# Sums of a norm taken as one-column matmuls, roots on 128x4 numbers, and their spreading over the partitions by transposes

## The chip, the cores and the metric

The kernel runs on one core of one Trainium2 chip. The metric is the device time of one execution in microseconds (us); the time quoted is the median of three executions. All data are 32-bit floats.

## The reference, cut to what matters

Two layers work on 256 context tokens and 256 latent tokens of width 1024. Each layer has two sub-layers, and each sub-layer ends in the norm of its own output, an addition to the stream, and the norm of the new stream:

```python
def rms_norm(x, g):
    y = x * lax.rsqrt(jnp.mean(jnp.square(x), axis=-1, keepdims=True) + 1e-6)
    return y * g

# end of the mixing sub-layer and start of the FFN sub-layer, for latent and context tokens alike
x = x + mod[2] * rms_norm(y, g_post_mix)
h = rms_norm(x, g_pre_ffn) * (1 + mod[4]) + mod[3]
# end of the FFN sub-layer and start of the next layer
x = x + mod[5] * rms_norm(conv_ffn(h), g_post_ffn)
h = rms_norm(x, g_pre_mix) * (1 + mod[1]) + mod[0]
```

In the second layer only latent tokens are needed after its mixing, so its boundaries work on 256 tokens and not on 512.

## The kernel before, in words

Activations are kept transposed: channels on the 128 partitions, tokens along the free dimension. The stream `x` is 8 tiles of 128 channels x 512 tokens, and so are `h` (as a high part `hh` and a low part `hl`) and the sub-layer's output. A projection goes over units of weights (512 KB each, one DMA of the SP queue into a ring of seven buffers). ACT rounds a unit to `whi` (`hi`, L443), DVE makes the rest `wlo` (`lo`, L842), and PE multiplies `whi` with both parts of the activations and `wlo` with the high part (`part`, L1499; in the first pairs after a boundary, where it follows the tiles of `h` one by one, `tile_part`, L1529). Two output tiles, a pair, stand in two banks of PSUM (banks 0 and 1, or 2 and 3) and are then evacuated.

A boundary is the end of the projection `out` or `down` and the start of the next projection. There are four: `out` and `down` of layer 0 (512 tokens), `out` of layer 1 (256 tokens), and the last, `down` of layer 1 (256 tokens), after which only the stream is stored. At each the kernel needs, for every token, sums over 1024 channels, that is, over partitions and over 8 tiles. With y the branch and s its scaled form, they are the sum of y squared, of s squared, and of x times s. From them it gets the root of the branch (`root1`), and with the sum of x squared from the boundary before (`ssum`) also the root of the new stream (`root2`), before the new stream exists:

    new sum = old sum + 2 * root * sum(x s) + root * root * sum(s s)

The order of each engine is written out by hand and is the program's order. Around a boundary it is:

- ACT (`evac_first`, then `boundary`) squares each pair, makes the branch with its gain (`branch`, L466) and its squares.
- DVE (`gather_sums`) forms x times s (`cross`, L939) and adds the tiles of three pairs and then the two halves of a tile to one (L959, L966). In `boundary` it adds the seventh tile to each of the three (L1029), splits one unit of weights (L842), and forms x times s of the eighth.
- PE (`last_pair`), after the last weights, takes the sums over partitions. `ones` (128x128) is the stationary operand and a tile of 128 channels x 512 tokens the moving one: one matmul for the seven tiles (`early_sum`, L1591) and one for the eighth (`last_sum`, L1598), for each of the three sums. The sum of every token then stands on all 128 partitions of a bank (6, 7 and 5). A matmul of 32-bit floats is run in two passes, so a view counts two MATMUL and two LDWEIGHTS for each. Five matmuls of 128x512 on the parameters follow (three in layer 1), whose results nobody reads (L1614).
- ACT makes the roots as Ln and Exp over 128x512 numbers (`root`, L555 and L556), DVE the new sum over 128x512 (L1057 to L1061), and ACT the second root.
- DVE then goes tile by tile: branch times root (`branch_tile`, L1014), added to the stream (`residual_tile`, L1019), stream times second root (`scaled_tile`, L1005), and later the low part of `h` (`low_tile`, L1010). ACT makes both forms of `h` behind it (L567), and PE starts the next projection with the first tile.

Of the kernel before, what the change touches and what calls it, by code (L numbers as in the profile page):

```python
# [134 lines left out]
def build(nc, xt, cvec, crow, weights, w_ada, w_ada_rows, w_gate, w_lr, w_dec, params, rope, out):  # L135
    with ExitStack() as ctx:
# [3 lines left out]
        def sem(name):  # L140
            return ctx.enter_context(nc.semaphore(name))
# [14 lines left out]
        ssum = sb("ssum", [P, TOK])  # L156
# [79 lines left out]
        root1 = {n: at(f"{n}_root", v[3], [P, TOK]) for n, v in SCRATCH.items()}  # L236
        root2 = {n: at(f"{n}_next_root", v[4], [P, TOK]) for n, v in SCRATCH.items()}
# [25 lines left out]
        s_sq, s_stat, s_r1, s_r2 = sem("squares_made"), sem("stat_done"), sem("root_made"), sem("next_root_made")  # L263
# [26 lines left out]
        s_tsq, s_tadd = sem("first_tile_squares"), sem("first_tile_added")  # L290
        s_c_gain, s_S0 = sem("first_gains_made"), sem("first_sum_copied")
# [141 lines left out]
        def _(act):  # L433
# [123 lines left out]

            def make_h(l, n, src, c0):
# [14 lines left out]
            def boundary(l, name):  # L573
# [17 lines left out]
                if not last:  # L591
                    wait_pair_taken(act, l, name, 3)
                    A_(scaled_squares[:, 1, c0:], branches[:, 1], ACT.Square).then_inc(s_sqp, 1)
                act.wait_ge(s_stat, m + 2)
# [13 lines left out]
            for l in range(DEPTH):  # L608
# [9 lines left out]
                if l == 0:  # L618
# [4 lines left out]
                    root(root2["down"][:], ps[:, 6], s_r2)  # L623
                    A_(ssum[:], ps[:, 6], ACT.Copy).then_inc(s_S0, 1)
# [208 lines left out]
        def _(dve):  # L833
# [166 lines left out]
            def scaled_tile(n, k, src, c0, root_):  # L1000
# [4 lines left out]
                V.tensor_tensor(src[:, k, c0:], x[:, k, c0:], root_[:, c0:], ALU.mult).then_inc(s_nt, 1)  # L1005
# [15 lines left out]
            def boundary(l, name):  # L1021
# [4 lines left out]
                def add_first_tile(j, ready_, count):  # L1026
                    v = sums_of[name][0][j][:, 0, c0:]
                    dve.wait_ge(ready_, count)
                    return V.tensor_tensor(v, v, sums_of[name][2][j][:, 0, c0:], ALU.add)  # L1029

                dve.wait_ge(s_acc, 2 * m + 2)
                if m == 2 * DEPTH - 1:
                    add_first_tile(0, s_tsq, 2 * m + 1).then_inc(s_tadd, 1)
                    dve.wait_ge(s_r1, m + 1)
                    for k in range(0, KT, 2):
# [3 lines left out]
                        V.tensor_tensor(two, two, root1[name][:, None, c0:].broadcast_to([P, 2, TOK - c0]), ALU.mult)\  # L1039
# [4 lines left out]
                n, root_ = m + 1, root1[name][:, c0:]  # L1044
                h0 = c0_of(l) if name == "out" else 0
                w = sums_of[name][0][0][:, 1, c0:]
# [8 lines left out]
                dve.wait_ge(s_r1, m + 1)  # L1055
# [3 lines left out]
                link(V.scalar_tensor_tensor(w, ps[:, 5, c0:], 2.0, w, ALU.mult, ALU.add))  # L1059
                link(V.tensor_tensor(w, w, root_, ALU.mult))  # L1060
# [28 lines left out]
            for l in range(DEPTH):  # L1089
# [14 lines left out]
                else:  # L1104
                    def scaled(k):
                        scaled_tile(0, k, nt0, 0, root2["down"])
# [884 lines left out]
```

## Time and profile before

| | |
|---|---|
| median of three executions | 1925.47 us (1924.86 to 1926.75) |
| the profiled execution's span | 1924.9 us, nothing before or after it counted |
| PE busy | 1858.9 us, 97% |
| weight loads (PEld) | 1545.5 us, 80% |
| DVE busy | 1343.7 us, 70% |
| ACT busy | 990.0 us, 51% |
| chain that ended last | PE 72%, DVE 18%, ACT 6%, issue 3% |
| DMA | 247.17 MB, mean 128 GB/s |

The profile gives for each group of instructions its line, engine, operation, output and inputs, shapes, number, busy time and mean duration, and the idle time of the engine just before, with what ended it. PE and PEld are the matmuls and the weight loads of the same engine; they overlap, and the ends of matmuls are modelled. Times in the views are microseconds from the start of the span. PEclk is the granted clock of PE as a share of full speed (1.00 is 2.4 GHz, 0.50 is 1.2 GHz).

### The profile page before, as it was taken

The page shows a single profiled execution, that of the slowest core. Times are in us where ns is not written, and L with a number is a line of the kernel's source. Part 1 is how long each engine was busy: PE and PEld are TensorE (multiplying, and loading weights), DVE is VectorE, ACT ScalarE, POOL GpSimd, SP SyncE. Part 2 cuts the span into 40 slices and gives each one's busy share as a digit, 9 for nine tenths or more (in the row PEclk, how much of TensorE's full clock was granted, in tenths as well). Part 3 has the DMA queues.
Part 4 walks back from the last instruction along what each step waited for, and adds up shares of the span by engine and source line. Part 5 has one row for each costly group of instructions (what it writes and reads, how often), then busy time and mean ns, then how long its engine had stood idle before and what let it go on. Part 6 is the DMA issues. An engine that isn't in the chain of part 4 may idle for free.

```text
span 1924.9 us, 26001 instructions
## 1 busy us (share of the span) xinstructions
PE 1858.9 (97%) x10504; PEld 1545.5 (80%) x10504; DVE 1343.7 (70%) x1934; ACT 990.0 (51%) x1405; POOL 18.9 (1%) x51
## 2 busy tenths in 40 slices
PE   7999999999999999899999998999999999989998
PEld 4778777777778887578888885778778888979997
DVE  5666546635677887878888797756556688678864
ACT  4543345555665323554444236543446887466663
POOL 1000000000000000000000000000000000000000
PEclk9999999999999999999999999999999999999999
DMA  8211212223244555234444563222323554535653
GB/s 340 70 56 56 72 55 66 77 82 97 90 142 132 181 190 186 98 103 150 164 164 152 188 218 108 77 66 66 93 66 99 155 162 150 183 114 186 181 182 120
DMA packets 68374, 247.17 MB, mean 128 GB/s; under 512 B 7696, under 2 KB 8736, under 8 KB 68128
## 3 DMA queue, kind: packets, MB, share of 16 engines
q1 hardware_dynamic: 65600, 235.96, 37.0%
q0 software_dynamic: 2080, 7.47, 1.3%
q10 hardware_dynamic: 576, 2.10, 0.3%
q8 instruction: 83, 1.36, 0.3%
q14 instruction: 35, 0.29, 0.0%
HBM read 244.44 MB, written 1.05 MB: 128 GB/s over the span
## 4 chain that ended last, share of the span: by engine, by line
PE 72%; DVE 18%; ACT 6%; issue 3%; POOL 0%; ACTq 0%; DVEq 0%; POOLq 0%
PE ps L1499 53%; DVE wlo L842 5%; PE ps L1489 4%; PE ps L1529 2%; DVE fa L892 2%; ACT whi L443 2%; PE ps L1774 2%; PE ps L1869 2%; PE ps L1795 1%; DVE state L1225 1%; PE ps L1707 1%; PE ps L1685 1%; DVE xc L892 1%; PE ps L1786 1%; PE ps L1646 1%
## 5 line engine op out<-in xcount | busy, mean ns | idle before, releaser
L842 DVE TENSOR_TENSOR wlo<-wraw,whi 128x1024 fp32r<-128x1024 f32 x352 | 429.5, 1222 | 235.0 <-ACT whi L443 234.6
L443 ACT ACTIVATE whi<-wraw 128x1024 fp32r<-128x1024 f32 x352 | 370.3, 1054 | 221.8 <-PE ps L1499 208.9
L1499 PE MATMUL ps<-hh,whi 128*128 128x512 f32 (+1 forms) x1632 | 369.3, 348 | 7.3 <-DVE fa L892 3.2
L1499 PE MATMUL ps<-hl,whi 128*128 128x512 f32 (+1 forms) x1632 | 366.0, 346 | 0.0
L1499 PE MATMUL ps<-hh,wlo 128*128 128x512 f32 (+1 forms) x1632 | 335.1, 346 | 1.9 <-DVE wlo L842 1.9
L1499 PEld LDWEIGHTS ps<-hh,whi 128*128 128x128 f32 x1632 | 269.6, 190 | 49.1 <-issue 9.1
L1499 PEld LDWEIGHTS ps<-hl,whi 128*128 128x128 f32 x1632 | 271.2, 190 | 37.6 <-issue 1.6
L1499 PEld LDWEIGHTS ps<-hh,wlo 128*128 128x128 f32 x1632 | 262.7, 190 | 41.1 <-issue 4.4
L870 DVE SCALAR_TENSOR_TENSOR ps<-wada,cond 128x1024 f32<-128x1024 f32 x144 | 173.4, 1246 | 0.0
L892 DVE SCALAR_TENSOR_TENSOR fa<-ps,par,fa 128x510 f32<-128x510 f32 (+1 forms) x176 | 100.1, 610 | 17.2 <-ACT fa L522 15.7
L1499 PE MATMUL ps<-bh,whi 128*128 128x512 f32 (+1 forms) x384 | 88.7, 353 | 0.0
L1499 PE MATMUL ps<-bl,whi 128*128 128x512 f32 (+1 forms) x384 | 82.1, 336 | 0.0
L522 ACT ACTIVATE fa<-ps,par 128x512 f32<-128x512 f32 (+1 forms) x88 | 54.0, 664 | 51.2 <-PE ps L1499 46.2
L1499 PE MATMUL ps<-fh,whi 128*128 128x512 f32 (+1 forms) x352 | 76.8, 336 | 1.2 <-ACT whi L443 1.2
L1499 PE MATMUL ps<-fl,whi 128*128 128x512 f32 (+1 forms) x352 | 76.6, 336 | 0.0
L1499 PEld LDWEIGHTS ps<-bh,whi 128*128 128x128 f32 x384 | 63.1, 190 | 14.6 <-issue 7.7
L1499 PE MATMUL ps<-bh,wlo 128*128 128x512 f32 (+1 forms) x384 | 74.4, 336 | 0.0
L722 ACT ACTIVATE probT<-ps 128x1024 f32<-128x1024 f32 (+1 forms) x24 | 21.2, 884 | 99.4 <-PE ps L1786 99.4
L1499 PE MATMUL ps<-fh,wlo 128*128 128x512 f32 (+1 forms) x352 | 69.5, 336 | 0.0
L1499 PEld LDWEIGHTS ps<-bl,whi 128*128 128x128 f32 x384 | 62.5, 190 | 7.5
L1499 PEld LDWEIGHTS ps<-bh,wlo 128*128 128x128 f32 x384 | 60.8, 190 | 7.5
L1499 PEld LDWEIGHTS ps<-fh,whi 128*128 128x128 f32 x352 | 57.6, 190 | 8.3 <-ACT whi L443 1.4
(300 smaller groups left out, 2592.7 us busy)
## 6 DMA issues: line engine op xcount, KB each, us to landing
wraw<-in_weights SPq DMA_DIRECT2D x352, 512.0 KB, 3.6
wada<-in_w_ada_rows SPq DMA_DIRECT2D x80, 512.0 KB, 3.5
ada_first<-in_w_ada SPq DMA_DIRECT2D x14, 512.0 KB, 16.3
wgate<-in_w_gate POOLq DMA_DIRECT2D x16, 256.0 KB, 2.9
x<-in_xt ACTq DMA_DIRECT2D x2, 512.0 KB, 7.7
x<-in_xt SPq DMA_DIRECT2D x2, 512.0 KB, 7.1
ada_first<-in_w_ada ACTq DMA_DIRECT2D x2, 512.0 KB, 12.5
wdec<-in_w_dec POOLq DMA_DIRECT2D x2, 512.0 KB, 4.8
```

Source lines behind the costliest of these rows:

```text
L443: A_(whi[u % HI][:], wraw[RING_W[u] % RAW][:], ACT.Copy).then_inc(s_hi, 1)
L522: ins = A_(fa[j][:, f, c0:], pair_[:, f, c0:], ACT.Identity, scale=pcol(l, "fw")[:, t + 2 * FT:t + 2 * FT + 1], bias=pcol(l, "fb")[:, t:t ...
L722: A_(probT[b][:, 0:2 * g + 2], ps[:, 6:8].rearrange("p a (b c) -> p (a b) c", c=SEQ)[:, 0:2 * g + 2], ACT.Copy).then_inc(s_ptc, 1)
L842: V.tensor_tensor(wlo[s][:], wraw[s][:], whi[u % HI][:].bitcast(F32), ALU.subtract).then_inc(s_lo, 1)
L870: ins = V.scalar_tensor_tensor(dst, w[:], 1.0, cond[:, s], ALU.mult, ALU.mult, accum_out=mod[:, layer, t, s:s + 1])
L892: return V.scalar_tensor_tensor(o[:, :, a], v[:, :, b], pcol(l, name)[:, tile:tile + 1], o[:, :, a], ALU.mult, ALU.add)
L1225: ins = V.scalar_tensor_tensor(state[:, d, p + 1], state[:, d, p], g_end[:, d, c:c + 1], kv_, ALU.mult, ALU.add)
L1489: ins = mm(dst[:, r // 2, 256 * (r % 2):256 * (r % 2 + 1)], x_[:, UK * h + kk, r * P:(r + 1) * P], w[:, kk, :], start=first, stop=h == m - ...
L1499: ins = mm(dst[:, r, c:], w[:, kk, r * P:(r + 1) * P], x_[:, UK * h + kk, c:], start=h == 0 and k in (0, 2) and kk == 0, stop=h == m - 1 a ...
L1529: ins = mm(dst[:, r, c:], w[:, kk, r * P:(r + 1) * P], x_[:, k, c:], start=k == 0 and part == 0, stop=k == KT - 1 and part == 2)
L1774: ins = mm(ps[:, 4 + t, 0:(g + 1) * CTX], aq[:, h, r0:r0 + P], ak[:, h // (AQ // AKV), 0:(g + 1) * CTX], start=True, stop=True)
L1869: ins = mm(ps[:, 4 + 2 * d + g], wgate[:, 2 * d + g, :], xc[:, n, :], start=True, stop=True)
```

## The change

The three sums are taken with the data as the stationary operand and one column of `ones` as the moving one. For 128 tokens each matmul gives 128x1 numbers, with tokens on partitions; 512 tokens give 128x4. Roots and the new sum are computed on 128x4 numbers (`rstat`). To bring a root back to all partitions, ACT writes it with its last Exp into 128 columns for each of four groups of tokens (`spread` on ACT, 128x512), and PE transposes the four 128x128 blocks into PSUM (`spread` on PE), banks 4 and 6, from where DVE reads it. DVE no longer adds the seventh tile; PE sums it apart. The unread matmuls on the parameters become two (`keep_on`), one behind each spread. At the kernel's start the sum of x squared is taken off the diagonal of bank 6 by DVE, where ACT copied it before. The last boundary needs one sum and one spread.

```diff
 # ACT
+            def spread(dst, i, t0):
+                return A_(dst[:, t0:], rstat[:, i, t0:, None].broadcast_to([P, TOK // P - t0, P]), ACT.Exp, scale=-0.5)
...
                 act.wait_ge(s_stat, m + 2)
-                root(root1[name][:, c0:], ps[:, 6, c0:], s_r1)
+                link(A_(rstat[:, 0, t0:], ps[:, 6, t0:TOK // P], ACT.Ln, scale=1.0 / D_MODEL, bias=eps[:]))
+                spread(root_rows[name], 0, t0).then_inc(s_r1, 1)
                 if not last:
+                    A_(rstat[:, 1, t0:], rstat[:, 0, t0:], ACT.Exp, scale=-0.5).then_inc(s_r1c, 1)
                     act.wait_ge(s_S, m + 1)
-                    root(root2[name][:, c0:], ssum[:, c0:], s_r2)
+                    link(A_(rstat[:, 3, t0:], ssum[:, t0:], ACT.Ln, scale=1.0 / D_MODEL, bias=eps[:]))
+                    spread(next_root_rows[name], 3, t0).then_inc(s_r2, 1)
...
-                    A_(ssum[:], ps[:, 6], ACT.Copy).then_inc(s_S0, 1)
 # DVE, scaled_tile
-                dve.wait_ge(s_r2, n + 1)
                 if n:
+                    dve.wait_ge(s_R2, n)
                     dve.wait_ge(s_x, KT * (n - 1) + k + 1)
+                else:
+                    dve.wait_ge(s_r0, 1)
+                root_ = ps[:, 6, c0:] if n else first_root[:, c0:]
 # DVE, branch_tile
-                V.tensor_tensor(src[:, k, c0:], src[:, k, c0:], root1[name][:, c0:], ALU.mult).then_inc(s_ym, 1)
+                dve.wait_ge(s_R1, m + 1)
+                V.tensor_tensor(src[:, k, c0:], src[:, k, c0:], ps[:, 4, c0:], ALU.mult).then_inc(s_ym, 1)
 # DVE, boundary
-                cross(l, name, 6, 7, sums_of[name][2][2]).then_inc(s_tadd, 1)
-                add_first_tile(0, s_tsq, 2 * m + 1)
-                add_first_tile(1, s_tsq, 2 * m + 2)
-                add_first_tile(2, s_tadd, 2 * m + 1).then_inc(s_tadd, 1)
+                cross(l, name, 6, 7, sums_of[name][2][2]).then_inc(s_x6, 1)
                 lo(LATE[m])
...
-                dve.wait_ge(s_r1, m + 1)
+                dve.wait_ge(s_r1c, m + 1)
                 dve.wait_ge(s_cs, m + 1)
-                link(V.tensor_tensor(w, ps[:, 7, c0:], root_, ALU.mult))
+                link(V.tensor_tensor(w, ps[:, 7, t0:TOK // P], r, ALU.mult))
                 dve.wait_ge(s_bs, m + 1)
...
-                V.tensor_tensor(ssum[:, c0:], w, ssum[:, c0:], ALU.add).then_inc(s_S, 1)
+                V.tensor_tensor(ssum[:, t0:], w, ssum[:, t0:], ALU.add).then_inc(s_S, 1)
 # PE
+            def column_sum(v, bank, l, start=False, stop=False):
+                for t in range(c0_of(l) // P, TOK // P):
+                    ins = mm(ps[:, bank, t:t + 1], v[:, t * P:(t + 1) * P], ones[:, 0:1], start=start and t == c0_of(l) // P,
+                             stop=stop and t == TOK // P - 1, skip_group_check=True)
+                return ins
             def early_sum(l, name, bank, j):
-                pe.wait_ge(s_tadd, 2 * m + (1 if m == 2 * DEPTH - 1 else 2))
-                mm(ps[:, bank, c0:], ones[:], sums_of[name][0][j][:, 0, c0:], start=True, stop=False)
+                pe.wait_ge(s_acc, 2 * m + 2)
+                column_sum(sums_of[name][0][j][:, 0], bank, l, start=True)
+                ready_, n = ((s_tsq, 2 * m + 1), (s_tsq, 2 * m + 2), (s_x6, m + 1))[j]
+                pe.wait_ge(ready_, n)
+                column_sum(sums_of[name][2][j][:, 0], bank, l)
             def last_sum(l, name, bank, j):
-                mm(ps[:, bank, c0:], ones[:], sums_of[name][2][j][:, 1, c0:], start=False, stop=True).then_inc(done, 1)
+                column_sum(sums_of[name][2][j][:, 1], bank, l, stop=True).then_inc(done, 1)
+            def spread(rows, bank, l, done):
+                for t in range(c0_of(l) // P, TOK // P):
+                    ins = nc.tensor.transpose(ps[:, bank, t * P:(t + 1) * P], rows[:, t], ident[:])
+                ins.then_inc(done, 1)
 # PE, last_pair, behind the last weights
-                for bank, j in banks:
+                early_sum(l, name, *SUM_BANKS[0])
+                last_sum(l, name, *SUM_BANKS[0])
...
+                for bank, j in SUM_BANKS[1:]:
                     early_sum(l, name, bank, j)
+                for bank, j in SUM_BANKS[1:]:
                     last_sum(l, name, bank, j)
...
+                pe.wait_ge(s_r1, m + 1)
+                spread(root_rows[name], 4, l, s_R1)
+                pe.wait_ge(s_par, 16)
+                keep_on(6, 1)
+                pe.wait_ge(s_r2, m + 1)
+                spread(next_root_rows[name], 6, l, s_R2)
+                pe.wait_ge(s_S, m + 1)
+                keep_on(7, 1)
```

PE's queue at the first boundary, from the last multiplication with weights to the first of the next projection, before (`ones` is the 128x128 tile of ones, `par` the parameters; x4 is four more of the same, and each is one matmul here, of two passes):

```order
L1499 MATMUL ps<-mh,wlo_64 128x512 x4
L1591 MATMUL ps<-out_squares_133,ones 128x512 [waits first_tile_added,ada_tiles_done]
L1598 MATMUL ps<-out_squares_139,ones 128x512 [waits squares_made]
L1591 MATMUL ps<-out_scaled_squares_134,ones 128x512 [waits first_tile_added]
L1598 MATMUL ps<-out_scaled_squares_140,ones 128x512 [waits scaled_squares_made]
L1591 MATMUL ps<-out_cross_135,ones 128x512 [waits first_tile_added]
L1598 MATMUL ps<-out_cross_141,ones 128x512 [waits cross_made]
L1614 MATMUL ps<-par,ones 128x512 [waits params_loaded]
L1614 MATMUL ps<-par,ones 128x512 x4
L1529 MATMUL ps<-hh,whi_81 128x512 [waits h_hi_made,w_hi_made,pair0_taken]
```

The same place in the changed kernel, from the first wait for the eighth tile on (12 matmuls of one column for each sum, of which four of the first sum stand above this; `root_rows` and `next_root_rows` hold the two roots, tokens on partitions):

```order
L1597 MATMUL ps<-ones,out_squares_139 128x1 [waits squares_made]
L1597 MATMUL ps<-ones,out_squares_139 128x1 x3
L1597 MATMUL ps<-ones,out_scaled_squares_134 128x1 [waits sums_added]
...
L1597 MATMUL ps<-ones,out_cross_141 128x1 [waits cross_made]
L1597 MATMUL ps<-ones,out_cross_141 128x1 x3
L1620 MATMUL ps<-ident,out_root_rows 128x128 [waits root_rows_made]
L1620 MATMUL ps<-ident,out_root_rows 128x128 x3
L1626 MATMUL ps<-par,ones 128x512 [waits params_loaded]
L1620 MATMUL ps<-ident,out_next_root_rows 128x128 [waits next_root_rows_made]
L1620 MATMUL ps<-ident,out_next_root_rows 128x128 x3
L1626 MATMUL ps<-par,ones 128x512 [waits next_sum_made]
L1536 MATMUL ps<-hh,whi_81 128x512 [waits h_hi_made,w_hi_made,pair0_taken]
```

Six matmuls became 36, the spreads of both roots stand behind all of them in PE's queue, and the unread matmul of bank 6 stands between the two spreads.

DVE's queue there in the changed kernel, behind the split of the unit of weights:

```order
L949 TENSOR_TENSOR out_cross_141<-x,mixed 128x512 [waits pair1_taken]
L1062 TENSOR_TENSOR rstat<-ps,rstat 128x4 [waits scaled_squares_summed,root_columns_made]
L1064 SCALAR_TENSOR_TENSOR rstat<-ps,rstat 128x4 [waits cross_summed,dve_chain]
L1065 TENSOR_TENSOR rstat<-rstat 128x4 [waits dve_chain]
L1066 TENSOR_TENSOR ssum<-rstat,ssum 128x4 [waits dve_chain]
L1028 TENSOR_TENSOR mixed<-mixed,ps 128x512 [waits root_spread]
L1033 TENSOR_TENSOR x<-x,mixed 128x512 [waits branch_scaled]
L1018 TENSOR_TENSOR mixed<-x,ps 128x512 [waits x_updated,next_root_spread]
```

The four operations on sums are the same four, with 4 columns in place of 512; the roots are read out of PSUM, and two waits for PE's transposes are new.

## Rows read from the trace of the kernel before

**Rows 1.** Stretches around the first boundary; columns: us, length, busy per engine, PEclk, DMA, GB/s

```profile
786.00:788.00 2.00, 0.32 (x2) 0.00 (x0) 2.00 (x4) 1.61 (x4) 0.00 (x0) 1.00 1.01 367
788.00:790.00 2.00, 1.57 (x2) 0.63 (x3) 2.00 (x3) 0.34 (x1) 0.00 (x0) 0.68 0.55 217
790.00:792.00 2.00, 2.00 (x4) 0.94 (x3) 0.02 (x1) 0.04 (x1) 0.00 (x0) 0.50 0.00 0
792.00:794.00 2.00, 2.00 (x5) 0.81 (x5) 0.10 (x1) 1.28 (x2) 0.00 (x0) 0.97 0.00 0
...
820.00:822.00 2.00, 2.00 (x6) 1.53 (x5) 1.32 (x3) 1.35 (x4) 0.00 (x0) 0.50 0.00 0
```

**Rows 2.** Timeline: last weights on PE before each of three boundaries; columns: start, us

```profile
785.25 1.07 PE L1499 MATMUL ps<-mh,wlo 128*128 128x512 f32 x4
...
1168.39 0.61 PE L1499 MATMUL ps<-fh,wlo 128*128 128x512 f32 x2
...
1705.02 0.64 PE L1499 MATMUL ps<-mh,wlo 128*128 128x256 f32 x4
```

**Rows 3.** Chain that ended last, first boundary (layer 0, out); columns: start, us

```profile
788.43 1.79 PE ps L1591 x2
...
794.66 0.87 PE ps L1598 x2
...
799.21 0.70 DVE mixed L1005
```

**Rows 4.** The same chain, second boundary (layer 0, down)

```profile
1173.63 0.87 PE ps L1598 x2
...
1177.53 0.64 ACT down_next_root L556
...
1178.19 0.70 DVE nt L1005
```

**Rows 5.** The same chain, third boundary (layer 1, out, 256 tokens)

```profile
1709.58 0.45 PE ps L1598 x2
...
1712.04 0.42 ACT out_next_root L556
...
1712.48 0.43 DVE mixed L1005
```

**Rows 6.** Timeline of the last boundary

```profile
1914.86 0.70 PE L1598 MATMUL ps<-down_squares,ones 128*128 128x256 f32 x2
1915.59 0.47 ACT L555 ACTIVATE down_root<-ps,eps 128x256 f32<-128x256 f32 x1 [0.42 <-PE ps L1598]
...
1916.62 0.69 DVE L1039 TENSOR_TENSOR y<-y,down_root 128x512 f32<-128x512 f32 x1 [3.38 <-ACT down_root L556]
```

**Rows 7.** Groups by form: weight loads of 32, 64 and 128 columns (PEld)

```profile
L1434 PEld LDWEIGHTS ps<-ada_first,csil 128*32 128x32 f32 x128 | 3.3, 109 | 3.9 <-issue 2.5
...
L1672 PEld LDWEIGHTS ps<-gl_qd,gl_ki 128*64 128x64 f32 x192 | 6.3, 137 | 2.6 <-issue 2.4
...
L1761 PEld LDWEIGHTS ps<-asq,ones 128*128 128x128 f32 x40 | 6.9, 189 | 6.5 <-ACT asq L699 5.4 <-issue 0.2
```

**Rows 8.** Chain: small matmuls and transposes in the scan branch of layer 0

```profile
75.07 1.09 PE ps L1672 x32
...
77.28 0.87 PE ps L1658 x8
```

**Rows 9.** Groups by form: small operations of ACT and DVE

```profile
L667 ACT ACTIVATE gstat<-gstat,eps 128x4 f32<-128x4 f32 x4 | 1.2, 297 | 0.1
...
L668 ACT ACTIVATE gstat<-gstat 128x4 f32<-128x4 f32 x4 | 0.8, 207 | 0.1
...
L876 DVE TENSOR_TENSOR mod<-mod,par 128x8 f32<-128x8 f32 x20 | 3.3, 167 | 0.7
```

**Rows 10.** Timeline at the start: two transposes, their reader, and DVE behind the first tiles

```profile
21.88 0.44 PE L1443 MATMUL ps<-ident,ada_rows 128*128 128x128 f32 x2 [0.55 <-DVE ada_rows L848]
...
22.35 0.17 DVE L854 TENSOR_REDUCE msum<-ps 128x4 f32<-128x16 f32 x1 [0.53 <-PE ps L1443]
...
57.83 1.23 DVE L842 TENSOR_TENSOR wlo<-wraw,whi 128x1024 fp32r<-128x1024 f32 x1 [3.51 <-ACT whi L443]
```

More of the change, by code:

```diff
@@ L622, in _ @@
                     act.wait_ge(s_stat, 1)
-                    root(root2["down"][:], ps[:, 6], s_r2)
-                    A_(ssum[:], ps[:, 6], ACT.Copy).then_inc(s_S0, 1)
+                    root(first_root[:], ps[:, 6], s_r0)
                     for u in range(LEAD):
@@ L1025, in boundary @@
                 src, dst = (mixed, mixed) if name == "out" else (y2, nt0)
[L1026 to L1029, printed above, removed]
                 dve.wait_ge(s_acc, 2 * m + 2)
                 if m == 2 * DEPTH - 1:
-                    add_first_tile(0, s_tsq, 2 * m + 1).then_inc(s_tadd, 1)
-                    dve.wait_ge(s_r1, m + 1)
+                    dve.wait_ge(s_R1, m + 1)
                     for k in range(0, KT, 2):
@@ L1038, in boundary @@
                             wait_pair_taken(dve, l, name, 3)
[L1039 removed]
+                        V.tensor_tensor(two, two, ps[:, 4, None, c0:].broadcast_to([P, 2, TOK - c0]), ALU.mult)\
                             .then_inc(s_ym, 2)
@@ L1585, in _, with keep_on @@
             SUM_BANKS = ((6, 0), (7, 1), (5, 2))
-            def early_sum(l, name, bank, j):
-                m, c0 = 2 * l + (name == "down"), c0_of(l)
-                pe.wait_ge(s_tadd, 2 * m + (1 if m == 2 * DEPTH - 1 else 2))
-                mm(ps[:, bank, c0:], ones[:], sums_of[name][0][j][:, 0, c0:], start=True, stop=False)
+            def column_sum(v, bank, l, start=False, stop=False):
[3 more added lines that the diff above has]
+                return ins
+            def early_sum(l, name, bank, j):
+                m = 2 * l + (name == "down")
+                pe.wait_ge(s_acc, 2 * m + 2)
[3 more added lines that the diff above has]
+                column_sum(sums_of[name][2][j][:, 0], bank, l)
             def last_sum(l, name, bank, j):
-                m, c0 = 2 * l + (name == "down"), c0_of(l)
+                m = 2 * l + (name == "down")
                 ready_, n, done = ((s_sq, 2 + m + 1, s_stat), (s_sqp, 4 * m + 4, s_cs), (s_xy, 4 * m + 4, s_bs))[j]
                 pe.wait_ge(ready_, n)
-                mm(ps[:, bank, c0:], ones[:], sums_of[name][2][j][:, 1, c0:], start=False, stop=True).then_inc(done, 1)
+                column_sum(sums_of[name][2][j][:, 1], bank, l, stop=True).then_inc(done, 1)
[3 more added lines that the diff above has]
+                ins.then_inc(done, 1)
+            def keep_on(bank, n):
+                for _ in range(n):
+                    mm(ps[:, bank, :], ones[:], par[:].rearrange("p l n -> p (l n)")[:, 0:512], start=True, stop=True)
             def last_pair(l, name):
                 u = LAST_UNIT[PAIR_AT[l, name, 3]]
-                banks = SUM_BANKS[:1 if 2 * l + (name == "down") == 2 * DEPTH - 1 else 3]
+                m = 2 * l + (name == "down")
                 steps = [(v, k) for ks in ((0, 1, 4), (2, 3, 5)) for v in (u - 1, u) for k in ks]
@@ L1607, in last_pair @@
                 pe.wait_ge(s_adat, len(ADA_MIX) if (l, name) == (0, "out") else len(ADA_TILE))
-                for bank, j in banks:
+                early_sum(l, name, *SUM_BANKS[0])
+                last_sum(l, name, *SUM_BANKS[0])
+                if m == 2 * DEPTH - 1:
+                    pe.wait_ge(s_r1, m + 1)
+                    spread(root_rows[name], 4, l, s_R1)
+                    return
+                for bank, j in SUM_BANKS[1:]:
                     early_sum(l, name, bank, j)
+                for bank, j in SUM_BANKS[1:]:
                     last_sum(l, name, bank, j)
-                if len(banks) == 3:
-                    pe.wait_ge(s_par, 16)
-                    for _ in range(5 if c0_of(l) == 0 else 3):
-                        mm(ps[:, 4, :], ones[:], par[:].rearrange("p l n -> p (l n)")[:, 0:512], start=True, stop=True)
+                pe.wait_ge(s_r1, m + 1)
+                spread(root_rows[name], 4, l, s_R1)
+                pe.wait_ge(s_par, 16)
[4 more added lines that the diff above has]
+                keep_on(7, 1)
             pe.wait_ge(s_ready, READY)
```

37 lines of the change are left out of this document (21 added, 16 removed).

## The prediction

> **What bounds the kernel now.** I first read the table of busy times: PE is busy 97% of the span and carries 72% of the chain. So a boundary counts only by how late PE gets its next real work, and I looked at the four boundaries and nowhere else. The chain of waits shows what stands there. At the first one PE is free at 786.32 (785.25 + 1.07) [rows 2], waits for DVE's additions, sums from 788.43 to 795.53, and the first scaled tile starts at 799.21 [rows 3]. At the second PE goes straight from the weights, free at 1169.00 [rows 2], into the sums, which end at 1174.50; the first scaled tile starts at 1178.19 [rows 4]. At the third PE is free at 1705.66 [rows 2], the sums end at 1710.03, the scaled tile starts at 1712.48 [rows 5]. Thus from the end of the sums to the scaled tile it takes 3.7, 3.7 and 2.5 us, all of it DVE and ACT on wide data. The last boundary has one sum; DVE starts on the result at 1916.62 [rows 6]. What follows a scaled tile is the same work before and after, so I price a boundary by the start of its first scaled tile.
>
> The second view is the clock. PE stood nearly idle at 786 to 788 (busy 0.32 of 2 us), and the granted clock then fell to 0.50 (1.2 GHz) and was back at 792 to 794 (0.97), after sums that streamed 512 columns each. It is at 0.50 again at 820 to 822, behind PE's wait for the last tile of `h` [rows 1]. The 1.28 us short in 788 to 790 put the fall at about 788.6, so that stretch lasts some 3.4 us and costs 1.7 us of full-speed work.
>
> **The change, priced.** The unknown is one pass of a one-column matmul: it loads 128x128 numbers as weights to move one column, which no row of before does. Weight loads of 32, 64 and 128 columns take 109, 137 and 189 ns [rows 7]. That is 0.83 ns a column, 107 ns for 128, above a fixed part that can overlap. Transposes, 128 columns loaded and 128 moved, follow each other every 109 ns (0.87 / 8) [rows 8]. I take 0.109 us. The low end is the 0.034 us of the small matmuls of 64 columns, whose loads run side by side in two halves of the array (1.09 / 32) [rows 8]. The high end is 0.19 us, a load that overlaps nothing [rows 7]. The price is nearest to the transposes, since width and size of the load are theirs. The Trainium skill, TensorE: Matmul & The Clock Gate, "Back-to-back issue gap", gives some 25 ns for a matmul of 1 to 64 columns; by it the sum would be that of the second rival below. The section on LDWEIGHTS of the same page sets a load by its columns alone, at P/1.2 ns, which speaks against this change.
>
> Three sums over 512 tokens are 36 such matmuls, 72 passes, 7.85 us; before they were 12 passes of 0.43 us (0.87 / 2 [rows 4]), 5.2 us. All 36 stand behind the last weights in PE's queue, so they are on the path. Then the tail: three linked DVE operations of 4 columns at 0.17 us and a wait of some 0.04 each, 0.64 us; ACT's Ln on 128x4, 0.30, and Exp into 512 columns, 0.64, with two waits, 1.0 us [rows 4, 9]; four transposes to their reader, 0.69 us (two take 22.35 - 21.88 = 0.47 [rows 10], two more 0.22). Together 2.33 us instead of 3.7. The third boundary has half of each width: 3.92 us, and a tail of 0.64 + 0.79 + 0.47 = 1.9 us with the Exp of 256 columns at 0.42 [rows 5].
>
> With the clock as it was before, the four come to:
> - First: 786.32 + 7.85 + 1.7 (the stretch at half clock) = 795.9, + 2.33 = 798.2 against 799.21: -1.0. DVE's three additions no longer hold PE up; that gain is in it.
> - Second: 1169.0 + 7.85 + 2.33 = 1179.2 against 1178.19: +1.0. Here PE never waited for DVE, and the longer sums cost more than the tail gives.
> - Third: 1705.66 + 3.92 + 1.9 = 1711.5 against 1712.48: -1.0.
> - Last: 12 passes for 4 of twice the length make the sum some 0.1 late, the Ln is 0.30 instead of 0.47 [rows 6, 9], the two transposes add 0.47: +0.4.
>
> Sum -0.6 us, no change at all. The small Exp of the root's columns (0.21 [rows 9]) is hidden behind the 48 passes that PE still has to do; with cheap passes it would cost its 0.2. The new DVE work at the start (two operations over 512 columns, about 1.3 us) stands where DVE next waits 3.51 us for ACT [rows 10]: 0. The copy that ACT drops there isn't on the chain: 0. DVE reading roots out of PSUM I cost at 0; if it were 0.03 us on each of 32 operations in the chain, it would be 1 us.
>
> Now the clock. The stream that brought it back is gone: what PE does from the last weights on moves single columns, and four of the unread matmuls are gone too, wherever the sums used to stream 512 columns. The likeliest, I think, is that such work doesn't hold the clock. Then at the first boundary 20 passes run before 788.5 and 52 at half speed, 11.3 us, to 799.8. Behind them in the same queue stand four transposes (0.87 at half speed) and the unread matmul (1.72), to 802.4, and only then the second spread, whose rows are ready at 801.4: 802.4 + 1.13 = 803.5, +4.3 against before. At the second boundary the fall should come some 4 us into the sums (it came 2.2 us after the weights at the first): 37 passes at full and 35 at half speed end at 1180.7, the queue behind them adds 3.7: 1184.4, +6.2 if so early, +5 if 1.2 us later; I take +5.5. At the third the sums are over by then and only the tail is slowed: -0.3 instead of -1.0. The last is too short: +0.4. Sum +9.9. Against it, each of three boundaries now ends in a stretch at half clock that costs 1.7 us [rows 1]; where it falls is moved by the change, and I let one and a half of them go, -2.5. Forecast +7.4 us. The same page of the Trainium skill, "Part 4: PE-mode transpose", says that transposes don't count as busy for the clock in the way that matmuls do; no row here shows a stretch of transposes alone, and by that rule the second spread would not bring it back either.
>
> **Rivals.**
> - The clock holds (a pass counts as work while its weights load). For it: PE's queue is never empty there, and the two unread matmuls sit in the gaps. Against: in all rows the clock is up where many columns move. Then -0.6, the 1.7 of the first stretch, and something of the closing stretches: about -3, 1922.5. Chance 0.20, a third of it over 0.2% faster.
> - The passes are cheap, and this is the case on the other side: loads of successive one-column matmuls overlap as they do for the 64-column ones [rows 8]. It decides below some 0.09 us. At 0.08 the boundaries come to -3.1, -1.1, -2.1 and +0.2, -6 in all; at 0.034 the sums end with their last operand and they come to about -7, -3.5, -2.8 and 0, -13. Against it: the slope of the loads [rows 7]. Chance 0.20, about 1917.
> - The loads overlap nothing, 0.19 us a pass: 13.7 us of sums, +4.9, +6.8, +1.9 and +1.2, +15 before any loss of clock. Chance 0.06, 1941 or more.
>
> **The numbers.** The forecast has 0.54: 1925.5 + 7.4 = 1933. The profiled span of 1924.9 stands 0.6 us below the median, so the difference can be laid on the median as it is. A measurement of this kernel can tell about 0.2%, 3.9 us, from no change. Its own range is 1929 to 1939. The range of all cases reaches from 1917 to 1939: it leaves out the third rival (0.06), the far ends of the second (0.06) and of the forecast (0.05). Faster by over 0.2%: 0.18 from the cheap passes and 0.07 from the clock that holds, 0.25. Within 0.2%: 0.13 + 0.02 and 0.06 from the low end of the forecast, 0.21. Slower: 0.54.
>
> **What would show it.** In the timeline after: the distance of one-column passes, 0.11 us at full and 0.22 at half clock; the clock at 0.50 through most of the sums of the first two boundaries; the second spread waiting for the unread matmul; first scaled tiles 4 to 6 us later against the last weights at the first two boundaries and about as before at the third; and in the last one 0.4 us. Passes under 0.09 us, or a clock at 1.00 through the sums, would make the forecast wrong, and the sums above say by how much.

## The result, and the profile after

The changed kernel takes 1935.45 us (median of 4 executions, 1934.6 to 1935.65), the kernel before beside it 1925.16 us (4 executions, 1923.61 to 1926.75): ratio 1.0053, 95% interval 1.0039 to 1.0067. That is 10.3 us slower, and the interval allows 7.5 to 12.9. The profiled execution took 1935.64 us, its span is 1933.5 us, 8.6 longer than the span of before. The forecast was 1933, slower. One execution among those reported below, of the kernel before with the new start alone, took 3086 us at a mean granted clock of 0.56, and the ratios leave it out.

By the page's table of busy times (engine, busy us, share, instructions) PE is 16.5 us busier than before with 160 more passes, and its weight loads are 25.2 us busier; DVE works 9.5 us less:

```profile
PE 1875.4 (97%) x10664; PEld 1570.7 (81%) x10664; DVE 1334.2 (69%) x1926; ACT 987.4 (51%) x1407; POOL 18.9 (1%) x51
```

PE's timeline at the first boundary (start, us, operation) shows the passes. It answers to [rows 2, 3]. All 72 passes of the three sums stand in it (eight of the first sum's 12 matmuls, and not four, stand above the queue shown with the change):

```profile
786.82 1.07 PE L1506 MATMUL ps<-mh,wlo 128*128 128x512 f32 x4
787.73 2.73 PE L1597 MATMUL ps<-ones,out_squares 128*128 128x1 f32 x24
790.33 1.93 PE L1597 MATMUL ps<-ones,out_scaled_squares 128*128 128x1 f32 x16
792.11 2.87 PE L1597 MATMUL ps<-ones,out_cross 128*128 128x1 f32 x16
...
796.55 1.85 PE L1597 MATMUL ps<-ones,out_cross 128*128 128x1 f32 x8
798.26 1.09 PE L1620 MATMUL ps<-ident,out_root_rows 128*128 128x128 f32 x4
799.15 1.91 PE L1626 MATMUL ps<-par,ones 128*128 128x512 f32 x2
800.85 1.06 PE L1620 MATMUL ps<-ident,out_next_root_rows 128*128 128x128 f32 x4
```

The first 24 passes take 2.60 us from start to start of the next group, 0.108 a pass; the 8 from 796.55 take 1.71, 0.214 each. The distance doubles where the clock halves, as the stretches of the same boundary show (us, length, busy time per engine, PEclk, DMA, GB/s), beside [rows 1]:

```profile
790.00:792.00 2.00, 2.00 (x20) 2.00 (x20) 0.00 (x0) 0.99 (x3) 0.00 (x0) 1.00 0.43 168
792.00:794.00 2.00, 2.00 (x16) 2.00 (x15) 0.00 (x0) 0.00 (x0) 0.00 (x0) 0.72 0.01 4
794.00:796.00 2.00, 2.00 (x11) 2.00 (x11) 0.00 (x0) 0.00 (x0) 0.00 (x0) 0.50 0.00 0
...
802.00:804.00 2.00, 1.46 (x3) 0.11 (x2) 1.93 (x3) 1.27 (x3) 0.00 (x0) 0.72 0.00 0
...
820.00:822.00 2.00, 0.55 (x2) 0.48 (x3) 1.89 (x4) 1.11 (x3) 0.00 (x0) 1.00 0.24 96
```

0.72 in the first and the last of the stretches is 1.12 us at 0.50 in each, so the clock is at 0.50 from 792.9 to 803.1, 10.2 us, though PE is never idle between the last weights and the scaled tile at 801.95. Before it was 3.4 us. The stretch that stood at 820 in [rows 1] is gone. At the second boundary the chain of waits (start, us, what) is the same story, against [rows 4]:

```profile
1170.16 10.48 PE ps L1597 x72
1180.64 0.96 PE ps L1620 x4
1181.60 1.71 PE ps L1626 x2
1183.30 0.87 PE ps L1620 x4
1184.17 0.02 issue
1184.19 0.70 DVE nt L1018
```

At the third, PE's timeline shows the fall inside the sums, after some 19 of the 36 passes (8 passes from 1713.66 take 0.99 us, the next 8 take 1.71), against [rows 5]:

```profile
1713.66 1.13 PE L1597 MATMUL ps<-ones,out_scaled_squares 128*128 128x1 f32 x8
1714.65 1.85 PE L1597 MATMUL ps<-ones,out_cross 128*128 128x1 f32 x8
1716.36 0.99 PE L1597 MATMUL ps<-ones,out_scaled_squares 128*128 128x1 f32 x4
...
1718.53 1.92 PE L1626 MATMUL ps<-par,ones 128*128 128x512 f32 x2
```

And the timeline of the last one, against [rows 6]:

```profile
1922.39 1.40 PE L1597 MATMUL ps<-ones,down_squares 128*128 128x1 f32 x12
...
1923.82 0.26 ACT L603 ACTIVATE rstat<-ps,eps 128x2 f32<-128x2 f32 x1 [0.49 <-PE ps L1597]
1924.12 0.41 ACT L563 ACTIVATE down_root_rows<-rstat 128x256 f32<-128x256 f32 x1
...
1925.16 0.69 DVE L1047 TENSOR_TENSOR y<-y,ps 128x512 f32<-128x512 f32 x1 [7.39 <-PE ps L1620]
```

Outside the boundaries one thing is new. From 24.9 to 28.3 us the clock is at 0.50, where it was at 1.00 before:

```profile
24.00:26.00 2.00, 1.12 (x4) 0.98 (x5) 2.00 (x4) 2.00 (x5) 0.00 (x0) 0.72 1.04 414
26.00:28.00 2.00, 2.00 (x12) 0.86 (x14) 0.80 (x3) 2.00 (x5) 0.00 (x0) 0.50 1.02 406
```

These times give a ledger of the 8.54 us by which DVE starts later on the last result (1925.16 against 1916.62). A boundary is measured from the start of the last weights on PE to the start of the first scaled tile:

| stretch | before | after | difference |
|---|---|---|---|
| start to first boundary | 785.25 | 786.82 | +1.57 |
| first boundary | 13.96 | 15.13 | +1.17 |
| between first and second | 369.18 | 367.59 | -1.59 |
| second boundary | 9.80 | 14.65 | +4.85 |
| between second and third | 526.83 | 527.73 | +0.90 |
| third boundary | 7.46 | 8.98 | +1.52 |
| between third and last | 201.50 | 201.25 | -0.25 |
| last boundary (to DVE's product) | 2.64 | 3.01 | +0.37 |

So the boundaries alone cost 7.9 us. Between first and second the closing half-clock stretch is missing (-1.59). Between second and third (+0.90) it is longer, 6.8 us from 1202.5 instead of 3.4, and there is another of 3.4 us from 1188.8. The second execution of this kernel, below, doesn't have that one and needs 527.95 us there, no less, so it cost nothing that shows.

### The profile page after: what moved, and what is told of

It reads as the page before. It is cut to its first block, busy times and chain, and to the rows that moved or that the text cites. A ratio compares the mean times of both kernels' runs of the same rounds, so it can differ in the third digit from the quotient of the medians.

```text
span 1933.5 us, 26313 instructions
## 1 busy us (share of the span) xinstructions
PE 1875.4 (97%) x10664; PEld 1570.7 (81%) x10664; DVE 1334.2 (69%) x1926; ACT 987.4 (51%) x1407; POOL 18.9 (1%) x51
## 4 chain that ended last, share of the span: by engine, by line
PE 75%; DVE 16%; ACT 6%; issue 3%; POOL 0%; ACTq 0%; DVEq 0%; POOLq 0%
PE ps L1506 54%; PE ps L1496 4%; DVE wlo L852 4%; PE ps L1536 2%; DVE fa L902 2%; ACT whi L446 2%; PE ps L1813 2%; PE ps L1908 2%; PE ps L1597 1%; PE ps L1834 1%; DVE state L1232 1%; PE ps L1746 1%; PE ps L1724 1%; DVE xc L902 1%; PE ps L1825 1%
```

## The experiments

Eleven runs of ten kernels, each timed in five rounds against the kernel before on the same chip; two of them repeat a kernel. The theory is that the one-column sums are slow by the clock: passes that move one column don't hold it. Its main rival is that waits and the number of short passes make it fall, whatever they move.

**128 columns a pass.** In `column_sum`, with the readers taking every 128th number:

```
-ins = mm(ps[:, bank, t:t + 1], v[:, t * P:(t + 1) * P], ones[:, 0:1], ...
+ins = mm(ps[:, bank, t * P:t * P + 128], v[:, t * P:(t + 1) * P], ones[:, 0:128], ...
-link(A_(rstat[:, 0, t0:], ps[:, 6, t0:TOK // P], ACT.Ln, ...
+link(A_(rstat[:, 0, t0:], ps[:, 6, c0::P], ACT.Ln, ...
```

> The changed kernel with the same 72 passes in the sums, but each moves 128 columns of ones instead of one (the result stands 128 times, and its readers take every 128th number). Theory A (single columns don't hold the clock; the sums are slow because the granted clock falls to 0.50 in them): the clock stays near 1.00 through the sums of the second and third boundary, and falls for 3.4 us at most at the first. A pass stays at about 0.109 us, since that is the time of its load. From the start of the last weights to the first scaled tile 12.9 us at the first boundary (1.07 + 7.85 + 1.7 + 2.33; 15.1 in the changed kernel), 10.8 at the second (14.65), 6.4 at the third (8.98): some 8.5 us in all, time near 1927 us. Theory B (the clock falls because PE waits or because so many passes are short, whatever they move): the clock falls as in the changed kernel, 10.2 us at 0.50 at either 512-token boundary, and the time stays within 2 us of it, near 1935. Theory C (load and moved columns of a pass don't overlap): a pass takes 0.2 us at full clock, and the time is 8 us or more above the changed kernel.

Measured 1925.72 us, ratio 0.9992 (0.9982 to 1.0001): 0.8 us below the kernel before, where the change stands 10.3 above. Two stretches of the second boundary and its chain:

```profile
1170.00:1172.00 2.00, 2.00 (x20) 2.00 (x19) 0.00 (x0) 0.56 (x2) 0.00 (x0) 1.00 0.64 254
1172.00:1174.00 2.00, 2.00 (x20) 2.00 (x19) 0.00 (x0) 0.00 (x0) 0.00 (x0) 1.00 0.02 8
```

```profile
1166.82 8.05 PE ps L1597 x72
...
1175.89 0.64 ACT down_next_root_rows L563
1176.52 0.04 issue
1176.57 0.67 PE ps L1620 x4
1177.24 0.02 issue
1177.26 0.70 DVE nt L1018
```

The same 72 passes take 8.05 us instead of 10.48, 0.112 each, and the clock stays at 1.00. The distance from weights to scaled tile is 11.51, 11.05 and 6.63 us at the three boundaries (15.13, 14.65, 8.98 in the change). From the end of the sums to the scaled tile it is 2.39. Theory A holds: the only thing changed in the sums is how much a pass moves. The second and third boundary are within 0.3 us of what was expected, and the first is 1.4 shorter, since no half-clock stretch fell into it. Moving 128 columns for one costs 0.004 us a pass (0.112 against 0.108). The distance of the passes hardly depends on what they move, so it must be set by what both have in common, the load.

**Streams between the sums.** The other way round: one-column sums, and behind each early sum an unread matmul:

```
+keep_on(4, 1)    # behind each early_sum, not at the last boundary
```

> The changed kernel, one-column sums and all, with one unread matmul of 512 columns behind each of the three early sums of a boundary (none at the last boundary). It adds work on the path, 0.86 us at full clock each, 2.6 us a boundary. Theory A (the clock goes by the columns that PE moves): with these streams the half-clock time at either 512-token boundary shrinks from 10.2 us to 3.4 or nothing, and the saved 32 passes at 0.218 pay for the streams: from the last weights to the first scaled tile 13.4 us at the second boundary (14.65 in the changed kernel), 14 to 15 at the first (15.1), 8.5 to 9 at the third (8.98), and less at half clock behind the scaled tiles: 1930 to 1934 us. Rival B (the clock falls by the start of the sums or by waits, whatever is moved): 10.2 us at half clock as before and the streams at 1.7 us each: 5 us more a boundary, 1945 us or more.

Measured 1941.93 us, ratio 1.0079 (1.0065 to 1.0093). A miss: slower than the change, and nearer to the rival's number. The second boundary:

```profile
1172.48 1.84 PE L1597 MATMUL ps<-ones,down_squares 128*128 128x1 f32 x16
1174.18 1.10 PE L1626 MATMUL ps<-par,ones 128*128 128x512 f32 x2
...
1177.71 1.64 PE L1626 MATMUL ps<-par,ones 128*128 128x512 f32 x2
1179.15 3.41 PE L1597 MATMUL ps<-ones,down_cross 128*128 128x1 f32 x16
```

```profile
1176.00:1178.00 2.00, 2.00 (x18) 1.99 (x18) 0.00 (x0) 0.99 (x3) 0.00 (x0) 1.00 0.45 180
1178.00:1180.00 2.00, 2.00 (x7) 1.19 (x5) 0.00 (x0) 0.00 (x0) 0.00 (x0) 0.54 0.00 0
```

The clock falls at 1178.2, 5.7 us after the start of the sums (5.2 in the change), though one stream has passed and one has begun by then, and the third, at half speed, takes 1.8 us. It stays at 0.50 for 13.7 us at either 512-token boundary (10.2 in the change), and these take 19.1 and 19.2 us to the scaled tile. At the third boundary, where a stream stands behind every 8 or 12 passes, it is otherwise:

```profile
1718.00:1720.00 2.00, 2.00 (x17) 1.79 (x16) 2.00 (x3) 1.65 (x4) 0.00 (x0) 1.00 0.59 229
1720.00:1722.00 2.00, 2.00 (x15) 1.72 (x14) 0.71 (x2) 0.87 (x4) 0.00 (x0) 1.00 0.74 254
```

Here the clock is at 1.00 through all the sums, which start at 1718.70, and the boundary takes 9.10 us, near the 8.5 to 9 of theory A. In both executions of the change the clock fell 2.1 us into the same sums. So the streams didn't hold the clock at the two long boundaries; at the short one it held, in a single trace, which doesn't show that they were the reason. Theory A was wrong on how little would do.

**Without the first unread matmul.**

```
-keep_on(6, 1)
```

> The changed kernel without the unread matmul between the two spreads. Theory A (it costs by its place in the queue: in the changed kernel the second spread starts at 800.85, when that matmul is done, while its rows are ready at 800.05): the second spread starts about 0.8 us earlier at both 512-token boundaries and some 0.4 at the third, about 2 us less in all, 1933.5 us. Rival B (it helps to bring the clock back): the half-clock stretches at the boundaries get longer by what it would have prevented, the work after the scaled tile is slower, and the time is equal or up to 3 us above the changed kernel.

Measured 1934.29 us, ratio 1.0042 (1.0028 to 1.0056). Stretches of its first boundary:

```profile
788.00:790.00 2.00, 2.00 (x15) 2.00 (x15) 0.28 (x1) 1.21 (x4) 0.00 (x0) 0.70 0.54 209
...
802.00:804.00 2.00, 1.65 (x3) 0.22 (x2) 1.86 (x4) 1.42 (x3) 0.00 (x0) 0.50 0.00 0
804.00:806.00 2.00, 2.00 (x5) 1.11 (x6) 1.89 (x3) 1.96 (x5) 0.00 (x0) 0.54 0.00 0
```

Both theories are true. The second spread starts 1.94 us after the first instead of 2.59, so the place in the queue cost 0.65 (0.8 expected). But the clock is at 0.50 for 17.1 us at either 512-token boundary. At the first it falls at 788.8, 2.8 us after the start of the sums, which makes that boundary 16.66 long. The second takes 14.41 (14.65 in the change). At the third the clock falls only behind the sums, and the boundary takes 6.84 instead of 8.98. The differences about cancel: 7.8 us above before lies between the two results of the change (10.3, and 6.8 below).

**The first tile added by DVE**, as in the kernel before, so that a bank sums two groups:

```
+add_first_tile(0, s_tsq, 2 * m + 1)
+add_first_tile(1, s_tsq, 2 * m + 2)
+add_first_tile(2, s_x6, m + 1).then_inc(s_tadd, 1)
...
-column_sum(sums_of[name][2][j][:, 0], bank, l)      # in early_sum
```

> The changed kernel with DVE's three additions of the first tile of the last pair put back, so that PE sums two groups a bank instead of three: 48 one-column passes instead of 72 at a 512-token boundary, 24 instead of 36 at the third, 8 instead of 12 at the last. Theory A (a boundary costs by its passes, 0.109 us at full and 0.218 at half clock): the 24 passes that go are those at half clock, so up to 5.2 us less at the second boundary and 2.6 at least, 1.3 to 2.6 less at the third; at the first PE waits for the additions some 2 us first, so only 0.5 to 3 less. In all 5 to 9 us less than the changed kernel, 1926.5 to 1930.5 us. Rival B (the fixed parts count, and the sums are hidden behind DVE's work on the last tile): within 1.5 us of the changed kernel, about 1935.

Measured 1931.08 us, ratio 1.0023 (1.0014 to 1.0032), 4.6 above before, where the change stands 10.3 and 6.8 above. A third of the passes is gone, and the time is just above the range expected, but the sizes at the boundaries were not as expected. PE's timeline at the second boundary:

```profile
1171.50 1.92 PE L1607 MATMUL ps<-ones,down_squares 128*128 128x1 f32 x16
1173.28 1.76 PE L1607 MATMUL ps<-ones,down_scaled_squares 128*128 128x1 f32 x8
...
1178.31 1.85 PE L1607 MATMUL ps<-ones,down_cross 128*128 128x1 f32 x8
```

Here the clock falls 1.9 us after the start of the sums and not 5.2, so 17 passes run at full speed and the other 31 at half, and the boundary takes 12.92 us, 1.7 less than in the change instead of 2.6 to 5.2. The first is even longer than in the change, 17.01: PE waits 2.1 us for the additions, and the clock falls at 787.7, before the sums begin. The third takes 7.20, 1.8 less, as expected.

**Both edits, 128 columns and the additions:**

> Both earlier edits at once: 128 columns a pass, and DVE adds the first tile, so 48 passes of 0.112 us. If the two effects add up: at the second boundary 11.05 - 24 x 0.112 + 0.3 = 8.6 us from the last weights to the scaled tile (9.8 in the kernel before), at the first the sums start 3.2 after the weights, when DVE has added: 3.2 + 5.4 + 2.7 = 11.3 (11.5 with three groups), + 1.7 if PE's wait makes the clock fall, at the third 6.6 to 6.8 as with three groups, at the last 2.8. So 2.5 us less than with 128 columns alone, about 1923.5 us. Rival B (the additions hold PE up at the second boundary too, or the clock falls in the wait of the first): 1925 us or more, no gain from fewer passes.

Measured 1922.06 us, ratio 0.9978 (0.9969 to 0.9988). The boundaries take 12.80, 8.70, 7.06 us and 2.93. The first is the 11.3 + 1.7 of the expectation, for the clock falls at 788.5, just behind PE's wait of 2.1 us; the second is 2.35 shorter than with three groups, so the passes saved show in full (24 x 0.112 = 2.7, less a later start of 0.26). The effects add up.

**A mixed version.** 128 columns a pass, the additions at the second boundary alone, the last boundary as in the kernel before:

```
+if m == 1: add_first_tile(...)       # and two groups a bank there
+if m == 2 * DEPTH - 1: (two wide sums, root on 256 columns in SBUF, no spread)
```

> A version put together boundary by boundary: 128 columns a pass; DVE adds the first tile at the second boundary alone, where PE doesn't wait for it; the last boundary as in the kernel before (two wide sums, roots on 256 columns in SBUF). If each boundary costs by its own parts: 11.5, 8.6, 6.6 and 2.64 us from the last weights to the first scaled tile (to DVE's first product at the last), against 13.96, 9.8, 7.46 and 2.64 in the kernel before: -2.5, -1.2, -0.8, 0, 4.5 us less, 1922 us, and 3 us below 128 columns alone. Rival B (what is gained at a boundary is given back by the clock behind it, as at the second one, where half-clock time grew from 3.4 to 6.8 us with 128 columns): 1.7 to 3.4 us of it are lost, 1924 to 1926.

Measured 1921.67 us, ratio 0.9978 (0.9969 to 0.9987), boundaries 11.51, 9.05, 6.62 and 2.64. The second is 0.35 longer than in the version before it: in the chain 0.40 us stand before DVE's second statistic operation, for which the profile names nothing. It was run again:

> The mixed version a second time, to see whether its gain stands: 4.5 to 5.5 us below the kernel before, ratio 0.997 to 0.998; if the first result was luck of the clock's phases, the two runs differ by 2 us or more, and the interval reaches 1.

Measured 1921.71 us, ratio 0.9980 (0.9972 to 0.9989), boundaries 11.50, 9.06, 6.63, 2.64. It beats both kernels, the one before by some 5 us and the change by 11 to 14. It isn't shown to beat the version with additions everywhere (1922.06): by the traces its boundaries are 1.7 us shorter in all, and the times can't tell that.

**128 columns without the unread matmul:**

> 128 columns a pass, without the unread matmul between the two spreads. In the changed kernel its removal moved nothing in all, because the second spread came 0.8 us earlier after it but the clock stayed at 0.50 for 6.8 us longer at both 512-token boundaries (17.1 instead of 10.2). Theory A (it matters as moved columns, and here the sums move enough): the clock holds through the sums, the spread wasn't held up by it (PE waited 0.41 us for its rows), and the time is that of 128 columns alone within 1 us. Rival B (it is what holds the clock between sums and products): a half-clock stretch of 3.4 us or more comes at the first boundary, where there was none, and the time is 2 us or more above.

Measured 1926.18 us, ratio 0.9998 (0.9989 to 1.0007), boundaries 11.57, 11.11, 6.69 and 3.12 (11.51, 11.05, 6.63 and 3.12 with it). The clock is at 1.00 through the whole first boundary. With 128 columns moved by each pass of the sums the unread matmul neither costs nor helps by anything that these times can tell.

**The kernel before without its unread matmuls:**

> The kernel before without its unread matmuls (5, 5 and 3 of 512 columns behind the sums), the other part of the change that takes moved columns away. They fill 4.3 of the 5.7 us in which PE waits for the first scaled tile. Theory A (columns moved hold the clock, over some microseconds): with nothing there the granted clock falls to 0.50 behind the sums at two or three boundaries, for 3.4 to 7 us each; since DVE and ACT set the pace of the first tiles behind it, only a part shows: 2 to 6 us above the kernel before, 1929 to 1932. Rival B (the sums alone, 5.2 us of streams, are enough): the clock stays as it was, and since the unread matmuls were off the path the time is the same within 1 us, 1926.5.

Measured 1927.47 us, ratio 1.0008 (0.9999 to 1.0017). The second boundary:

```profile
1176.00:1178.00 2.00, 0.00 (x0) 0.00 (x0) 1.93 (x4) 0.32 (x1) 0.00 (x0) 1.00 0.00 0
1178.00:1180.00 2.00, 0.00 (x0) 0.00 (x0) 1.84 (x4) 1.15 (x3) 0.00 (x0) 0.73 0.00 0
1180.00:1182.00 2.00, 0.88 (x3) 0.81 (x4) 1.78 (x4) 1.96 (x4) 0.00 (x0) 0.50 0.00 0
```

With PE idle behind the sums the clock does fall, for 6.8 us at either 512-token boundary, as theory A says; but the time rises by 1.1 us, not by 2 to 6, and the interval goes from no difference to 3.3 us. PE has slack there: in these stretches DVE, busy 1.78 to 1.93 of 2 us, sets the pace of the tiles. So the seven unread matmuls that the change drops of the 13 (three at each 512-token boundary, one at the third) are not what makes it slow: without all 13 the kernel before loses 1.1 us, and the change loses 7 to 10. A clock at half counts where PE's queue is full, which in the change is in the sums.

**The start alone.** The kernel before with the start of the changed one:

```
-A_(ssum[:], ps[:, 6], ACT.Copy).then_inc(s_S0, 1)
...
-dve.sem_inc(s_gain, 1)
+V.tensor_copy(attm[:, 0], ps[:, 6])
+V.tensor_copy(ssum[:], ps[:, 6]).then_inc(s_gain, 1)
```

> The kernel before with the start of the changed one alone: ACT's copy of the first sums is dropped, and DVE does two operations over 512 columns in its place, after the last low tile (the second makes the same copy, so that all boundaries are as before). In the trace of the changed kernel the granted clock is at 0.50 from 24.4 to 27.8 us, where it was at 1.00 before, and the first boundary is reached 1.57 us later. Theory A (the change at the start causes this): the half-clock stretch near 24 us is there, and the time is 1.6 us above that of the kernel before, 1927 us. Rival B (the phase of the clock's fall is luck of one execution): no such stretch, time within 0.5 us of before; and then the runs that share the changed kernel's start show the stretch in some and not in others.

Measured 1926.08 us, ratio 0.9998 (0.9989 to 1.0007), the clock at 1.00 near 25 us. The start costs nothing that can be measured, and the stretch there is chance: two traces with the changed start have it (the change, 128 columns), nine others with the same start don't, and the kernel before without its unread matmuls, whose start is that of before, has it:

```profile
24.00:26.00 2.00, 0.94 (x3) 0.69 (x4) 2.00 (x4) 2.00 (x5) 0.00 (x0) 0.81 1.02 406
26.00:28.00 2.00, 2.00 (x12) 0.93 (x15) 1.08 (x4) 2.00 (x5) 0.00 (x0) 0.50 1.04 414
```

In the same way the stretch inside the first boundary of before [rows 1] is chance: with the start alone that boundary takes 12.26 us, and without the unread matmuls, where all code up to the end of its sums is that of before, 12.27, instead of 13.96. Against 12.27 the first boundary of the change costs 2.9 us, and not the 1.17 of the ledger.

**The changed kernel again:**

> The changed kernel a second time, beside the mixed version on one chip. Its four runs stood 10.3 us above the kernel before. 8.6 of it are in the profiled execution's span, of which 1.6 came from a half-clock stretch near 24 us that two of four kernels with the same start don't show. If that stretch is luck and counts here, the median of more runs is 8 to 10 us above before, 1934.5 to 1936; if the start costs 1.6 each time, it isn't below 10.

Measured 1933.15 us, ratio 1.0043 (1.0031 to 1.0055), 6.8 above before, so below the range that was expected. The stretch near 25 us isn't there, and the boundaries are the same to 0.15 us: 15.06, 14.51, 8.91 and 3.01. The clock falls 5.2 and 5.3 us into the first two sums and 2.1 into the third, as in the first execution. The last weights before the first boundary start at 784.29 instead of 786.82, so some 2.5 us of the first trace were the luck of the start (1.6 against the trace of before). The change costs 7 to 10 us.

## Why the prediction was right, and where it was not

The direction, the mechanism and the size of the sum were right (+7.4 predicted, +10.3 and +6.8 measured), but some steps made up for each other, so that the sum came out so near is in part luck.

- **The pass.** 0.109 us was taken, from the transposes [rows 8]; 0.108 was measured at full clock and 0.214 at half. Of the rivals, the cheap passes (below 0.09) and the loads that overlap nothing (0.19) both fall. The Trainium skill (TensorE: Matmul & The Clock Gate, "Back-to-back issue gap") gives its 25 ns for 1 to 64 columns as the gap of a single matmul, and says that in a stream of pairs of load and matmul both set the spacing. The trace agrees with the second: with a new load for each pass the distance is 108 ns, and so the 25 ns were the wrong figure to set beside this sum.
- **The tail.** 2.33 us from the end of the sums to the scaled tile; 2.39 with the clock held. Reading the roots from PSUM costs DVE nothing that shows: 0.68 to 0.69 us an operation as before.
- **Sums without loss of clock.** The prediction's +1.0, -1.0 and +0.4 at the second, third and last boundary are +1.25, -0.83 and +0.48 with 128 columns a pass. At the first, 11.25 us were reckoned without the 1.7 of the stretch, and 11.51 measured, so these 1.7 us were priced from a stretch that only the one trace of before has.
- **The clock.** It falls in sums of one-column passes and would not if they moved 128: shown by the 128-column run, in which it holds and the time stands 0.8 us below the kernel before instead of 7 to 10 above. The rival by which the clock holds is out. The prediction also laid the loss of clock to four unread matmuls that are gone. It is three at each 512-token boundary, and they aren't the reason: the change has two left at each, and the 128-column run, with the same two, keeps the clock.
- **The first boundary was sized wrong:** +4.3 predicted, +1.17 measured. The step that failed took the fall of the clock from before, at 788.5; it came at 792.9. So about 47 passes ran at full speed and 25 at half, not 20 and 52, and 27 passes at 0.106 us are 2.9 of the 3.1 us that are missing. The moment isn't fixed by this code alone: it came 2.8 us after the start of the sums without the unread matmul, whose place is behind them, and 5.2 in both executions of the change.
- **The second was right:** +5.5 predicted, +4.85 measured; the fall at 1175.2 lies 5.2 us into the sums, and 4 to 5.2 had been assumed. No row gave these 4 us (the only fall on record came 2.2 us after the weights), so the size here rests on a guess that came true. The spread waited for the unread matmul, as said.
- **The third was wrong in sign:** -0.3 predicted, +1.52 measured. The step said that its sums would be over before the clock fell. It fell after some 19 of the 36 passes, 2.1 us into them, in both executions of the change. In the run without the unread matmul it fell after them and the boundary took 6.84, 0.62 less than before, so the step holds for that variant and fails for the change.
- **What was to be given back** was -2.5, for one and a half closing stretches. Only one went (-1.59), and what lies between the second and third boundary grew by 0.90; with the -0.25 before the last it is -0.9. That miss and the start (+1.57, at which nothing was reckoned) took the place of what the first boundary cost less.

What stays open is what decides when the clock falls in such sums: two executions of the change agree within 0.2 us, variants of it go from before the sums to 6.2 us into them, and the runs show no cause for it.

## What to carry to other kernels

Price a small matmul by the load of its weights, and then ask what it moves: if the load takes 0.11 us anyway, let the pass move 128 columns, which is nearly free here, and with which the clock stayed up through the sums in all five runs that did so, but for one stretch of 3.4 us behind a wait of PE. A reduction that puts tokens on partitions makes everything behind it small (2.4 us instead of 3.7), but it multiplies passes, so first shrink what must be summed on an engine that has slack. And where the clock falls matters only by what PE still has in its queue: before costing a half-clock stretch, look whether PE or another engine sets the pace in it.

## What was not expected of the hardware

- PE busy for 2.00 of each 2 us, with a weight load in flight all the time, still loses its clock where each pass moves one column; the same passes with 128 columns kept it, at 0.112 instead of 0.108 us a pass.
- Streams of 512 columns, 0.9 us each and one after every 16 or 24 one-column passes, didn't prevent the fall; it came 5.7 and 6.2 us after the start of the sums instead of 5.2. With one after every 8 or 12 the clock was at 1.00 throughout, in one trace.
- A half-clock stretch of 3.4 us near 25 us, and one inside the first boundary, come and go between executions of code that is the same up to there. The one inside the boundary is worth 1.7 us; the three traces with the one near 25 us reach the first boundary at 786.8 to 787.2 us, the ten without it at 784.1 to 785.3; a ledger from one execution each carries that much chance at every boundary, and the executions of the 128-column kernel lie in two bunches, four of eleven at 1920.7 to 1921.1 and six at 1925.7 to 1926.8.
